# A streaming encoder layer: value rows in four buffers, a Strassen operand in its own memory, and another order of loads

## What is computed

```
xn = rms_norm(x, attn_norm)
q, k, v, xl, yg, gl = split(xn @ w_in)           # 16 query heads, 4 key/value heads of 64
q, k = partial_rope(rms_norm(q)), partial_rope(rms_norm(k))
o = window_attention(q, k, v, sinks)
attn_branch = o @ w_attn_out
h = rg_lru(conv(xl)); lru_branch = (h * gelu(yg)) @ w_lru_out
g_a, g_b = split(sigmoid(gl))
x = x + (g_a * attn_branch + g_b * lru_branch) @ w_o
gate, up = split(rms_norm(x, ffn_norm) @ w_gate_up)
x = x + (silu(gate) * up) @ w_down
```

## Time and profile before

| | us |
|---|---|
| median of 3 runs | 1673.92 (1670.12 to 1674.09) |
| profiled execution | 1669.02 |
| its span | 1667.2 |
| TensorE busy | 1615.4 (97%) |
| VectorE busy | 1009.1 (61%) |
| GpSimd busy | 944.5 (57%) |
| ScalarE busy | 625.7 (38%) |

### The profile page before, as it was taken

The page is one execution under the profiler, slowest core; times in us unless marked ns, Lnnn a source line. Parts: engine busy times, 40 slices in busy tenths (PEclk is TensorE's granted clock), DMA queues, the critical chain, the costliest instruction groups (busy, mean ns, idle before and its releaser), DMA issues. The chain is left out here.

```text
span 1667.2 us, 28466 instructions
## 1 busy us (share of the span) xinstructions
PE 1615.4 (97%) x11270; PEld 1536.9 (92%) x11270; DVE 1009.1 (61%) x1718; ACT 625.7 (38%) x1294; POOL 944.5 (57%) x685
## 2 busy tenths in 40 slices
PE   7999998999999999999898999999999999999999
PEld 4899998989989898898897989999999999998998
DVE  6676555855545555857888787333333334869595
ACT  5535551253343425414334343333333333433232
POOL 4545552313212230568875709777777777786876
PEclk9999999999999999999999999999999999999999
DMA  5111222313122130364343412222242222473643
GB/s 182 47 51 64 64 76 88 91 56 113 61 96 69 67 118 31 117 246 169 134 151 103 155 59 84 78 77 78 77 181 78 77 79 76 146 281 117 240 145 147
DMA packets 73032, 182.09 MB, mean 109 GB/s; under 512 B 15092, under 2 KB 26676, under 8 KB 72260
## 3 DMA queue, kind: packets, MB, share of 16 engines
q1 hardware_dynamic: 52228, 160.35, 27.7%
q10 hardware_dynamic: 20672, 19.93, 3.8%
HBM read 131.23 MB, written 49.28 MB: 108 GB/s over the span
## 5 line engine op out<-in xcount | busy, mean ns | idle before, releaser
L597 PE MATMUL bank<-xh,wsh 128*128 128x264 f32 x2170 | 622.7, 287 | 21.5 <-POOL wsl L573 8.3
L597 PE MATMUL bank<-xh,wsl 128*128 128x264 f32 x2170 | 618.8, 285 | 0.0
L597 PE MATMUL bank<-xl,wsh 128*128 128x264 f32 x2170 | 618.2, 285 | 0.0
L597 PEld LDWEIGHTS bank<-xh,wsh 128*128 128x128 f32 x2170 | 410.4, 189 | 25.1 <-issue 15.5
L597 PEld LDWEIGHTS bank<-xl,wsh 128*128 128x128 f32 x2170 | 410.6, 189 | 0.3
L597 PEld LDWEIGHTS bank<-xh,wsl 128*128 128x128 f32 x2170 | 410.6, 189 | 0.0
L597 PE MATMUL bank<-acth,wh 128*128 128x352 f32 x960 | 318.7, 332 | 6.0 <-POOL wl L524 3.6
L597 PE MATMUL bank<-acth,wl 128*128 128x352 f32 x960 | 314.8, 328 | 0.0
L597 PE MATMUL bank<-actl,wh 128*128 128x352 f32 x960 | 313.6, 327 | 0.0
L522 POOL TENSOR_SCALAR wh<-wraw 128x512 fp32r<-128x512 f32 (+1 forms) x100 | 72.4, 724 | 396.1 <-PE bank L597 374.4
L573 POOL TENSOR_TENSOR wsl<-praw,wsh 128x512 fp32r<-128x512 f32 (+1 forms) x157 | 243.8, 1553 | 82.8 <-ACT wsh L1212 82.7
(11 more groups left out here) (179 smaller groups left out, 2308.7 us busy)
## 6 DMA issues: line engine op xcount, KB each, us to landing
praw<-in_weights SPq DMA_DIRECT2D x34, 1024.0 KB, 4.9
wraw<-in_weights SPq DMA_DIRECT2D x52, 512.0 KB, 3.3
h_scratch<-ev SPq DMA_DIRECT2D x44, 264.0 KB, 2.0
acc<-h_scratch SPq DMA_DIRECT2D x4, 2112.0 KB, 12.7
ev<-x_scratch SPq DMA_DIRECT2D x6, 1056.0 KB, 5.0
spare<-x_scratch SPq DMA_DIRECT2D x6, 1056.0 KB, 5.0
praw<-in_weights SPq DMA_DIRECT2D x8, 768.0 KB, 5.2
ta_scratch<-tg ACTq DMA_DIRECT2D x24, 176.0 KB, 1.9
```

What stands on the lines that cost most here:

```text
L597: return nc.tensor.matmul(*args, **kw)
```

## The change

It has four parts.

1. `vst` has four buffers and each its own semaphore, so copy t waits for the store of copy t-4. The ninth job's stores and that of `tail` stand behind the second key block's copy and square instead of ahead of the first.
2. The tile T2 of `LRU_OUT` leaves `spare` for `t2raw`, which shares its memory with `xl6`. `part_low` of part 6 then works in place and waits for the last product of pair 0. The load of `res[1]` for pair 1 moves from pair 1 to pair 0 in SyncE's order and loses its wait for the input parts.
3. `load_x(ATTN_OUT)` moves behind `load_pair(3)`. At the start of `ATTN_OUT` the gate rows of `res[0]` are loaded ahead of the last store of the LRU branch.
4. `rows_in` becomes `row_in(p, b)`: VectorE waits for the row of the buffer that it is about to read, and for that of `res[1]` only ahead of L1751.

```diff
-            vst = tensor(s, "vst", [P, 2, KVH * HD])
+            vst = tensor(s, "vst", [P, 4, KVH * HD])
...
-        for k in range(4, PRODUCTS):
+        for k in range(4, 6):
             x_slot(k)
+        xh.append(tensor(ctx, "xh6", [P, KQ, HALF], f32r))
+        with ExitStack() as raw:
+            t2raw = tensor(raw, "t2raw", [P, KQ, HALF])
+        xl.append(tensor(ctx, "xl6", [P, KQ, HALF], f32r))
...
-            return fifth if t == LRU_OUT else quarter(t, 0, 1)
+            return t2raw[:, :, :] if t == LRU_OUT else quarter(t, 0, 1)
...
-                if t >= 2:
-                    act.wait_ge(v_stored[t % 2], 16 * (t // 2))
-                f(vst[:, t % 2, :], bank[job.bank][:, 0:KVH * HD], ACT.Copy).then_inc(free[job.bank], 1)
+                if t >= 4:
+                    act.wait_ge(v_stored[t % 4], 16 * (t // 4))
+                f(vst[:, t % 4, :], bank[job.bank][:, 0:KVH * HD], ACT.Copy).then_inc(free[job.bank], 1)
                 if t >= 1:
                     store_v(t - 1)
-            store_v(8)
-            act.wait_ge(tail_done, 6 * GROUPS)
-            act.dma_start(tail_out, tail[:, :, :]).then_inc(stored, 16)
...
                 qk_copy(j // 6 * 6, j % 6, (kgain, qgain)[j // 6])
+                if j == 1:
+                    store_v(8)
+                    act.wait_ge(tail_done, 6 * GROUPS)
+                    act.dma_start(tail_out, tail[:, :, :]).then_inc(stored, 16)
                 if 1 <= j < 7:
                     k_root(j - 1)
...
                 dve.wait_ge(xhi_done, nth_high(t, k))
+                if t == LRU_OUT and k == 6:
+                    dve.wait_ge(mm_done, ended(0, 6))
...
-            def rows_in(p):
-                for b, n in res_loads(p).items():
-                    dve.wait_ge(res_in[b], n)
+            def row_in(p, b):
+                dve.wait_ge(res_in[b], res_loads(p)[b])
...
                 if r == 4:
-                    rows_in(p)
+                    row_in(p, b)
...
                 if r != 4:
-                    rows_in(p)
+                    row_in(p, b)
...
+                    row_in(p, 1)
                     dst = half if i == 0 else acc[:, 2 * i + m, toks(h)]
                     V.tensor_tensor(dst, half, res[1][:, m, toks(h)], ALU.add).then_inc(merged, 1)
...
-                    load_res(0, tiles(tb_dram, 0))
+                    for b in range(2):
+                        load_res(b, tiles(tb_dram, b))
                     return
-                if p == 1:
-                    x_unused(LRU_OUT)
-                    load_res(1, tiles(tb_dram, 1))
                 store_mb(p - 1)
                 if p + 1 < PHASE_FIRST[ATTN_OUT]:
                     sp.wait_ge(mb_stored[(p - 1) % 2], 16)
                     load_res((p + 1) % 2, tiles(tb_dram, p + 1))
-                if p == 1:
-                    load_x(ATTN_OUT)
...
                 if i == 0:
+                    sp.wait_ge(mb_stored[0], 32)
+                    load_res(0, tiles(ta_dram, i))
                     store_mb(p - 1)
-                    for b in range(2):
-                        sp.wait_ge(mb_stored[b], 32)
-                else:
-                    sp.wait_ge(merged, MERGED_LRU + 4 * i)
+                    sp.wait_ge(mb_stored[1], 32)
+                    load_res(1, tiles(mb_dram, i))
+                    return
+                sp.wait_ge(merged, MERGED_LRU + 4 * i)
                 load_res(1, tiles(mb_dram, i))
...
                 if p + 2 < N_PAIRS:
                     load_pair(p + 2)
+                if p == 1:
+                    load_x(ATTN_OUT)
```

More of the change, by code:

```diff
@@ L377, in build @@
         x1sq = spare[:, T:T + 3 * QB].rearrange("p (n t) -> p n t", t=QB)
-        fifth = spare[:, :].rearrange("p (c t) -> p c t", t=HALF)
         def qsquares(g):
@@ L454, in build @@
         one_done, b_done, h_done, prod_done = sem("lru_first_mult"), sem("lru_b"), sem("lru_h"), sem("lru_product")
-        v_stored, kv_stored, cs_loaded = [sem(f"v_stored{i}") for i in range(2)], sem("kv_stored"), sem("rope_loaded")
+        v_stored, kv_stored, cs_loaded = [sem(f"v_stored{i}") for i in range(4)], sem("kv_stored"), sem("rope_loaded")
         ss_done, copied, std_done = sem("k_sumsq"), sem("qk_copied"), sem("k_std")
@@ L1037, in store_v @@
                 if t < 8:
-                    act.dma_start(v_dram[t * P:(t + 1) * P, :], vst[:, t % 2, :]).then_inc(v_stored[t % 2], 16)
+                    act.dma_start(v_dram[t * P:(t + 1) * P, :], vst[:, t % 4, :]).then_inc(v_stored[t % 4], 16)
                 else:
-                    act.dma_start(v_dram[SEQ:T, :], vst[P - DEC:P, t % 2, :]).then_inc(v_stored[0], 16)
+                    act.dma_start(v_dram[SEQ:T, :], vst[P - DEC:P, 0, :]).then_inc(v_stored[0], 16)
                     act.dma_start(vs_out[WINDOW - DEC:WINDOW, :], vst[P - DEC:P, 0, :]).then_inc(stored, 16)
                 if t == 7:
-                    act.dma_start(vp_out[:, :], vst[:, 1, :]).then_inc(stored, 16)
+                    act.dma_start(vp_out[:, :], vst[:, 3, :]).then_inc(stored, 16)
             vjobs = []
@@ L1111, in _ @@
                 if j == 6:
-                    act.wait_ge(v_stored[0], 16 * 5)
-                    act.wait_ge(v_stored[1], 16 * 4)
+                    act.wait_ge(v_stored[0], 16 * 3)
+                    for i in range(1, 4):
+                        act.wait_ge(v_stored[i], 16 * 2)
                     act.wait_ge(stored, 16 * 3)
                 qk_copy(j // 6 * 6, j % 6, (kgain, qgain)[j // 6])
+                if j == 1:
+                    store_v(8)
+                    act.wait_ge(tail_done, 6 * GROUPS)
+                    act.dma_start(tail_out, tail[:, :, :]).then_inc(stored, 16)
                 if 1 <= j < 7:
@@ L2075, in _ @@
                 sp.wait_ge(mb_stored[i], 16 * 2)
-                sp.wait_ge(v_stored[i], 16 * (5 - i))
                 sp.wait_ge(ot_stored[i], 16 * 2)
@@ L2081, in _ @@
             sp.wait_ge(x1_stored, 16 * PAIRS[OUT])
+            sp.wait_ge(v_stored[0], 16 * 3)
+            for i in range(1, 4):
+                sp.wait_ge(v_stored[i], 16 * 2)
             sp.wait_ge(stored, 16 * (4 + 3))
```

## The result

The changed kernel takes 1660.88 us, the median of four runs (1660.03 to 1663.72). Four runs of the kernel before beside them have the median 1674.01 us. The ratio is 0.9932, with a 95% interval of 0.9914 to 0.995: 8 to 14 us faster (13.1 by the medians, 11.4 by the ratio). The profiled execution took 1660.03 us, with a span of 1658.1.

What follows compares the result with a forecast made beforehand. TensorE, busy 97% of the span, bounds the kernel. Terms 4.65 + 4.0 + 3.5 + 1.0 + 0.6 = 13.8 us, taken from the runs' median 1673.9, give 1660 us; range 1654 to 1667.

Steps and rivals of the forecast that it cites:

- Place B: First branch projection, pairs 0 to 3 and entry of pair 4: TensorE's waits and slow clock go, 9.1 us.
- Rival 4: Attention input, behind the weights and sharing with stores, arrives after 743 and delays three engines; slower than before; chance 0.02.
- rival 3: One place fails: pair 3's weights still wait in SyncE's queue, 8 us gained; or Place A fails, 9 us; chance 0.09.
- Part 2, 4.0 us: Pair 2: VectorE's wait for gate rows, TensorE's 2.17 us wait and 1.7 us of slow clock go, 4.0 us.
- Part 3, 3.5 us and 1.0 at pair 4: Weights ahead of input: pair 3's waits for GpSimd go, 3.5 us; pair 4's wait for VectorE goes, 1.0 us.
- Part 4, 0.6 us: Pair 4: VectorE's 0.57 us wait before its first gated product, taken for the rows' transfer, goes; 0.6 us.
- Place A: End of value projection: TensorE's gap before the key sums goes, partly returned at group 0's start; net 4.65 us.
- gross 7.15 us: Key sums: 5.26 us of gap and 1.89 us of slow block behind it go with four value buffers.
- give-back at the query sums: Start of group 0: VectorE comes only 4.5 us earlier, so 2.5 us return as waits for banks and squares.
- the 3 us beyond which the prediction called itself wrong: Sign of error: VectorE's run from second key block to last query copy differs from 40 us by over 3.
- rival 2: Waits return at query sums with lower clock, leaving 2.0 to 3.0 us; pair 4 gives 1.6 less; 1664 us; chance 0.20.

Runs made afterwards that it cites:

- late burst: Changed kernel with each group's query sums still one burst of 34 tiny matmuls, but behind the 36th dense matmul instead of the 18th: 1655.97 us, ratio 0.9896.

## Why the prediction was right, and where its steps were not

The forecast was 1660, the median is 1660.88. The sum was 13.8 us, 13.1 were measured beside it by medians. The parts did not add up as forecast.

- **Place B, 9.1 us forecast.** Measured 9.4 by medians, 10.2 between the two traces (9.7 to 11.5 over all pairs of traces). Right, and the rows are those announced: no wait and full clock at pair 2, weights ahead of the input, no wait for GpSimd in pair 3, pair 4 entered without a wait. Rival 4 is out, since the input was not late, and so is rival 3 in its first form.
- **Part 2, 4.0 us.** 3.9 in the trace, the weights being ahead.
- **Part 3, 3.5 us and 1.0 at pair 4.** The step that failed in attribution. The stalls of pair 3 were put down to the order of the queue ("issued at 726.08 behind 4 MB of the next input"). Behind the same 4 MB, but 9 us earlier, the weights made nobody wait. The queue was late since SyncE stood in the wait for the input parts, which part 2 had already removed. On top of part 2 the order is worth 0.0 us, not 3.5 and 1.0; without part 2 it is worth 5.0. Parts 2 and 3 each rescue pair 3; together they give 8.9 us where I had 8.5, and only because I counted the stalls once did the sum hold.
- **Part 4, 0.6 us.** Not settled. With part 2 and the order undone the measure is 196.45. The three traces of before's second half lie 0.8, 1.9 and 2.0 us above it, and that scatter is wider than the term. The earlier gate rows of pair 4 are in the difference too, and no run parted the two. VectorE's wait ahead of its first gated product (0.57 us before) is gone in the changed kernel.
- **Place A, 4.65 us net.** 0.7 us by medians, between -1.5 and 2.0. Three terms were off. The gross 7.15 us was there in the two profiled executions (7.0 us of lead), but not in every one: with the two old buffers the same gap was 1.54 us in one of four traces. The give-back at the query sums was 4.2 us for 2.5 forecast (7.0 - 2.84): VectorE's block started at 276.33 (forecast 277.0), but its run was 43.0 us instead of 40.4 (just inside the 3 us beyond which the prediction called itself wrong). The text had kept the length "and let it move by a few us"; that move was the cost. And the wait was followed by a burst at the lower clock (5.77 us for 3.83). That is rival 2's mechanism, and it was under-priced: it left 1.13 us, not 2.0 to 3.0. Run singly, the places come out as rival 3's second form had it (place A fails, 9 us): 10.1.
- **What no step had.** The bursts of query sums bring the lower clock in nearly every group, and how much of it a single execution shows is chance. Spread and later, the sums of the kernel before cost 12.7 us less by medians; 5.6 of these are in the traces. The forecast carried the profiled execution's sum over to the median, as if all that parts them were unchanged. Here it was nearly so. The median of 1674.0 lies 0.6 to 2.4 us above those of the later batches, and the two places give 10.1 us when run singly. Part of the agreement with 13.1 is luck, then: place B was better by up to 1 us and place A worse by 4.

The Trainium skill (GPSIMD Engine Reference, Key points) has GpSimd and VectorE contend for SBUF. The rows agree: the same VectorE operation of 128x352 takes 0.53 us and 1.49, and GpSimd's copy 0.62 and 0.89, where they meet. I had seen nothing that would change how many instructions meet; by the rows above a shift of 0.5 us between the engines does, and costs 2.6 us of VectorE's run.

Open: why the value stores land some 3.5 us sooner in one execution, how often they do, what parts the two clusters of runs with part 2 undone, and why a burst of tiny matmuls keeps the clock in 4 of 28 cases.

## What to carry to other kernels

Before a stall is put down to a transfer's place in a queue, ask when the queue itself was free: if a wait upstream goes, the order may not matter, and two edits can be worth the same stall only once. A lead on the bounding engine is worth what the engine that it waits for next lets through, and that engine's run must be taken as a range when a third engine slows it where their instructions meet and the change shifts the two. And put short matmuls between long ones, not in a burst: here the same work, spread and placed later, was worth as much as the whole change. Last, compare the granted clock of like stretches over several traces before reading a difference of two spans.

## What the runs showed of the hardware

- The granted clock falls at bursts of 34 matmuls of two columns, 3.8 us long where it holds, with no idle time behind them and, but for group 0 of four kernels, none ahead: in 24 of 28 cases from 2.4 to 1.2 GHz, for 3.4 us (11 cases), 6.8 us (12) or 13.7 us (one, from within the wait of 2.73 us ahead of the burst). In the others it falls 1.7 to 5.1 us after the burst begins. The same matmuls two at a time between dense ones keep it at 2.4 GHz, in 27 of 28. The Trainium skill (TensorE: Matmul & The Clock Gate, What's actually happening) says that the gate goes by "how busy the PE has been recently"; by the busy time of the profile, 20.00 of 20 us in the windows above, there would have been no fall. The measurement decides: the profile's busy time does not tell when the clock falls.
- Two tiny matmuls cost about the same spread as in the burst: 34 tiny and 30 dense matmuls together take 8.80 us, against 8.64 in the one late burst that kept the clock.
- Of seven value copies that each wait for a store the last starts at 272.96 in one execution and at 269.02 in another, 24.4 and 21.0 us after the first copy, with the same issues around them. In the changed kernel the first store of four still took 8.7 us from issue (249.02) to the copy that waited for it (257.75).
